# The opening of a decoder trunk in halves: the first conditioning group holds shift and scale of tiles 0 to 3, two weight units do half their products on it, and x is requested ahead of the conditioning weights

## What is computed

```python
def adaln(c, w, b):
    m = jax.nn.silu(c) @ w + b
    return m.reshape(c.shape[0], N_SUB, 3, c.shape[-1])     # shift, scale, gate of each sub-layer
def modulated(x, g, mod, s):
    h = rmsnorm(x, g)
    return h * (1 + mod[:, s, 1][:, None]) + mod[:, s, 0][:, None]
def half_ffn(x, g, mod, s, w_gu, w_down):
    return x + 0.5 * mod[:, s, 2][:, None] * swiglu(modulated(x, g, mod, s), w_gu, w_down)
```

## Time and profile before

| | |
|---|---|
| median of 3 runs | 1281.07 us (1280.49 to 1281.17) |
| profiled execution | 1282.18 us, of which the span from first to last instruction 1280.4 us |
| PE busy | 1231.6 us, 96% of the span |
| DVE, ACT, GpSimd busy | 667.7, 526.6, 131.3 us |
| mean granted TensorE clock | 0.992 |
| read from HBM | 266.55 MB |

### The profile page before, as it was taken

How to read it: one execution, slowest core, us unless ns; L and a number is a source line. 1 busy time by engine, 2 the same in 40 slices (tenths; PEclk the granted TensorE clock), 3 DMA queues, 4 the chain that set the end, 5 groups by cost and what they waited for, 6 DMA issues and landing times.

```text
span 1280.4 us, 23693 instructions
## 1 busy us (share of the span) xinstructions
PE 1231.6 (96%) x9979; PEld 1145.8 (89%) x9979; DVE 667.7 (52%) x986; ACT 526.6 (41%) x722; POOL 131.3 (10%) x124
## 2 busy tenths in 40 slices
PE   5899999999999999999999999999899899999997
PEld 2799999989998999999899999987677499999997
DVE  1644454566675445445545545558645356555553
ACT  1533333343444534333544433355534235554332
POOL 3000001210040000023000001310111040000031
PEclk9999999999999999999999999999999999999998
DMA  9777554568675774355677544584377372544442
GB/s 363 284 292 273 200 218 161 181 203 293 228 281 202 295 288 173 124 171 174 256 263 290 189 139 160 178 310 147 133 284 276 132 263 102 187 163 163 137 158 82
DMA packets 68711, 269.45 MB, mean 210 GB/s; under 512 B 4704, under 2 KB 5152, under 8 KB 54416
## 3 DMA queue, kind: packets, MB, share of 16 engines
q1 hardware_dynamic: 35664, 184.57, 40.0%
q10 hardware_dynamic: 29792, 59.09, 12.6%
q0 software_dynamic: 3168, 24.52, 5.2%
HBM read 266.55 MB, written 1.62 MB: 209 GB/s over the span
## 4 chain that ended last, share of the span: by engine, by line
PE 89%; DVE 4%; DMA 2%; ACT 2%; SPq 1%; issue 0%; ACTq 0%; POOL 0%; DVEq 0%; POOLq 0%
PE bank L1274 25%; PE bank L1275 24%; PE bank L1276 24%; PE bank L1320 3%; PE bank L1560 3%; DMA ada_early<-in_w_ada 1%; PE bank L1573 1%; PE bank L1612 1%; PE bank L1341 1%; ACT w_hi L604 1%; DVE w_lo L825 1%; DMA stage<-in_w_ci 1%; PE bank L1485 1%; DMA stage<-in_w_uq 1%; PE bank L1576 1%; PE bank L1481 1%
## 5 line engine op out<-in xcount | busy, mean ns | idle before, releaser
L825 DVE TENSOR_TENSOR w_lo<-stage,w_hi 128x2048 fp32r<-128x2048 f32 (+2 forms) x182 | 375.0, 2062 | 296.4 <-ACT w_hi L604 295.9
L1274 PE MATMUL bank<-h_hi,w_hi 128*128 128x288 f32 x1608 | 477.5, 297 | 2.8 <-DVE w_lo L825 1.9
L1276 PE MATMUL bank<-h_hi,w_lo 128*128 128x288 f32 x1608 | 475.1, 295 | 0.0
L1275 PE MATMUL bank<-h_lo,w_hi 128*128 128x288 f32 x1608 | 474.5, 295 | 0.0
L604 ACT CAST w_hi<-stage 128x2048 fp32r<-128x2048 f32 (+2 forms) x182 | 304.1, 1674 | 247.8 <-PE bank L1276 171.6
L1274 PEld LDWEIGHTS bank<-h_hi,w_hi 128*128 128x128 f32 x1608 | 302.1, 188 | 7.4 <-issue 3.7
L1275 PEld LDWEIGHTS bank<-h_lo,w_hi 128*128 128x128 f32 x1608 | 302.1, 188 | 0.0
L1276 PEld LDWEIGHTS bank<-h_hi,w_lo 128*128 128x128 f32 x1608 | 302.0, 188 | 0.0
L1275 PE MATMUL bank<-gu_lo,w_hi 128*128 128x288 f32 x768 | 226.6, 295 | 0.0
L1276 PE MATMUL bank<-gu_hi,w_lo 128*128 128x288 f32 x768 | 226.4, 295 | 0.0
L1274 PE MATMUL bank<-gu_hi,w_hi 128*128 128x288 f32 x768 | 225.3, 293 | 0.0
(11 more groups left out here) (233 smaller groups left out, 972.8 us busy)
## 6 DMA issues: line engine op xcount, KB each, us to landing
stage<-in_w_gu SPq DMA_DIRECT2D x88, 1024.0 KB, 4.9
stage_ada<-in_w_ada ACTq DMA_DIRECT2D x53, 1024.0 KB, 9.4
stage<-in_w_down SPq DMA_DIRECT2D x64, 704.0 KB, 4.0
stage<-in_w_ci SPq DMA_DIRECT2D x16, 768.0 KB, 4.5
stage_ada<-in_w_ada SPq DMA_DIRECT2D x9, 1024.0 KB, 10.3
ada_early<-in_w_ada SPq DMA_DIRECT2D x4, 1024.0 KB, 15.0
stage<-in_w_co SPq DMA_DIRECT2D x4, 1024.0 KB, 6.4
stage<-in_w_wo SPq DMA_DIRECT2D x4, 1024.0 KB, 4.9
```

The lines of the kernel that those rows point to most:

```text
L825: nc.vector.tensor_tensor(w_lo[part][:, 0:cols], stage[st_][:, 0:cols], w_hi[part][:, 0:cols], ALU.subtract).then_inc(lo_ready, 1)
L1274: nc.tensor.matmul(out, hi, x_hi, start=start, stop=False)
L1275: nc.tensor.matmul(out, hi, x_lo, start=False, stop=False)
L1276: return nc.tensor.matmul(out, lo, x_hi, start=False, stop=stop)
```

## The change

Group 0 now holds shift and scale of tiles 0 to 3, and group 1 those of tiles 4 to 7. Each quarter comes as two transfers of 512 KB (`half_quarter`), and DVE adds the bias in two instructions a group. x is requested ahead of all conditioning weights, both first weight units ahead of group 1's quarters 0 and 1. The sums of squares and the spread stand between the quarters of group 0 on PE, and the table of the root is loaded early on ACT (`any_root`). `first_norm`, the splits of units 0 and 1, and their products are done in two halves of 4 tiles: the first between group 0 and group 1, the second behind group 1.

```diff
+        def half_quarter(half, q):
+            units = a["w_ada"][0:2 * C_TILES].rearrange("(s u) p (q n) -> p s u q n", s=2, q=RING)
+            return [units[:, s, half * C_TILES // 2:(half + 1) * C_TILES // 2, q, :] for s in range(2)]
...
             sp.dma_start(consts[:], a["consts"]).then_inc(consts_in, 16)
+            sp.dma_start(x[:], a["x"]).then_inc(x_in, 16)
+            def load_half(half, q, into):
+                for s_, src in enumerate(half_quarter(half, q)):
+                    sp.dma_start(by_run(into[q])[:, 2 * s_:2 * s_ + 2], src).then_inc(half_loaded[half][q], 16)
             for q in range(RING):
-                sp.dma_start(by_run(ring[q]), quarter(0, q)).then_inc(ada_loaded[q], 16)
-                if q == 0:
-                    sp.dma_start(x[:], a["x"]).then_inc(x_in, 16)
+                load_half(0, q, ring)
             for q in range(RING):
-                sp.dma_start(by_run(ada_early[q]), quarter(1, q)).then_inc(early_loaded[q], 16)
-                if q == 1:
-                    sp.dma_start(stage[0][:, 0:FLAT[0]], a["w_gu"][0]).then_inc(loaded[0], 16)
+                if q < 2:
+                    sp.dma_start(stage[q][:, 0:FLAT[q]], a["w_gu"][q]).then_inc(loaded[q], 16)
+                load_half(1, q, ada_early)
...
@@ ScalarE @@
-            run("ada_first")
             act.wait_ge(setup_done, 2)
+            nc.scalar.activation(any_root[:], eps[:], ACT.Sqrt)
             root(0)
-            split_hi(0, FLAT[0], 0, 0, 16, False)
-            run("ada_second")
+            after(alone_steps(act, "ada_first")[0])
+            split_half(0, 0)
+            first_norm(0)
+            split_half(0, 1)
+            split_half(1, 0)
+            split_half(1, 1)
+            after(alone_steps(act, "ada_second")[0])
+            first_norm(1)
...
@@ VectorE @@
-            run("ada_first")
             square_last(0)
             inverse_root(0)
-            nc.vector.tensor_tensor(h_fp[:], x[:], rstd.unsqueeze(1).broadcast_to([P, KT, T]), ALU.mult)\
-                .then_inc(hs_step, 1)
-            split_lo(0, FLAT[0], 0, 0)
-            run("ada_second")
+            for half, done in enumerate((half_step, hs_step)):
+                tiles = slice(KT // 2 * half, KT // 2 * (half + 1))
+                nc.vector.tensor_tensor(h_fp[:, tiles], x[:, tiles], rstd.unsqueeze(1)
+                                        .broadcast_to([P, KT // 2, T]), ALU.mult).then_inc(done, 1)
+            after(alone_steps(dve, "ada_first")[1])
+            first_norm(0)
+            split_half(0, 1)
+            split_half(1, 0)
+            split_half(1, 1)
+            after(alone_steps(dve, "ada_second")[1])
+            first_norm(1)
...
@@ TensorE @@
+            def first_units(half):
+                tiles = range(KT // 2 * half, KT // 2 * (half + 1))
+                pe.wait_ge(hs_hi_ready if half else half_hi, 1)
+                for k, st in enumerate(list(steps(pe, SEG["ffn0_gu"], peel_first=True))[0:2]):
+                    pe.wait_ge(lo_ready if half else w_half_lo, k + 1)
...
+                    if k == 0:
+                        pe.wait_ge(hs_ready if half else half_lo, 1)
+                        mm = lagged(outs, parts, tiles, 0)
+                    else:
+                        for kt in tiles:
+                            for g in range(2):
+                                mm = three(outs[g], *parts(kt, g), h_hi[:, kt, :], h_lo[:, kt, :], kt == 0, kt == KT - 1)
+                    if half:
+                        mm.then_inc(unit_used, 1)
...
-            run("ada_first")
-            stats(0)
-            run("ada_second")
+            one_, two_ = alone_steps(pe, "ada_first"), alone_steps(pe, "ada_second")
+            ada_products(one_[0], range(0, 2))
+            stats_sums(0)
+            ada_products(one_[0], range(2, 3))
+            spread(0)
+            ada_products(one_[0], range(3, RING))
+            products(one_[1])
+            first_units(0)
+            products(two_[0])
+            products(two_[1])
+            first_units(1)
```

More of the change, by code:

```diff
@@ L399, in build @@
         loaded = [sem(f"loaded{s}") for s in range(STAGES)]
-        early_loaded = [sem(f"early_loaded{q}") for q in range(RING)]
+        half_loaded = [[sem(f"half_loaded{half}_{q}") for q in range(RING)] for half in range(2)]
         ada_loaded = [sem(f"ada_loaded{q}") for q in range(RING)]
@@ L625, in by_coef, with split_half, first_norm @@
                 nc.scalar.mul(h_fp[:, kt, 0:TP], x[:, kt, 0:TP], coef[:, kt, 0:1]).then_inc(scaled, 1)
+            def split_half(k, half):
+                cols = slice(UNIT // 2 * half, UNIT // 2 * (half + 1))
+                act.wait_ge(loaded[k], 16)
+                nc.scalar.copy(w_hi[k][:, cols], stage[k][:, cols]).then_inc(hi_ready if half else w_half_hi, 1)
+            def first_norm(half):
+                for kt in range(KT // 2 * half, KT // 2 * (half + 1)):
+                    if kt % (KT // 2) == 1:
+                        act.wait_ge(hs_step if half else half_step, 3)
+                        tiles = slice(KT // 2 * half, KT // 2 * (half + 1))
+                        nc.scalar.copy(h_hi[:, tiles, TP:T], h_fp[:, tiles, TP:T])\
+                            .then_inc(hs_hi_ready if half else half_hi, 1)
+                    act.wait_ge(normed, kt + 1)
+                    nc.scalar.activation(h_hi[:, kt, 0:TP], h_fp[:, kt, 0:TP], ACT.Identity,
+                                         bias=mods[:, kt, 0:1]).then_inc(h_hi_ready, 1)
             def norm(n):
@@ L887, in prompt_lo @@
                                                    op0=ALU.add, op1=ALU.subtract).then_inc(h_ready, 1)
[L889 to L893, removed]
-                    .then_inc(hs_step, 1)
[L895 to L900, removed]
+                first = tiles.start
+                dve.wait_ge(step, 1)
+                prompt(first)
+                nc.vector.tensor_tensor(hs4, hs4, by_seq(coef[:, tiles, 1:1 + NSEQ]), ALU.mult).then_inc(step, 1)
+                dve.wait_ge(step, 2)
+                nc.vector.tensor_tensor(hs4, hs4, by_seq(scale_shift(0)[:, tiles, 0, 1:1 + NSEQ]), ALU.add)\
+                    .then_inc(step, 1)
+                if half == 0:
+                    split_half(0, 0)
+                prompt_lo(first)
+                dve.wait_ge(hs_hi_ready if half else half_hi, 1)
+                nc.vector.tensor_tensor(h_lo[:, tiles, TP:T], h_fp[:, tiles, TP:T], h_hi[:, tiles, TP:T], ALU.subtract)\
+                    .then_inc(hs_ready if half else half_lo, 1)
+                for kt in range(first + 1, tiles.stop + 1):
+                    if kt < tiles.stop:
                         prompt(kt)
-                    if kt > 1:
+                    if kt > first + 1:
                         prompt_lo(kt - 1)
@@ L1053, in _ @@
                     norm(n)
-                else:
-                    first_norm()
                 if n == 0:
-                    split_lo(1, FLAT[1], 1, 1)
                     dve.wait_ge(tables_in, 16 * N_TABLES)
```

78 lines of the change are left out of this document (56 added, 22 removed).

## The result

The changed kernel takes **1288.46 us** (median of 5 runs, 1286.9 to 1289.18) where the kernel before takes 1281.17 (5 runs, 1280.49 to 1281.76). The ratio is 1.0058 with a 95% interval from 1.0047 to 1.0068: 7.3 us lost. The forecast was 1285.4, with a range up to 1287.3. Direction and mechanism came as forecast, the size did not.

What follows compares the result with a forecast made beforehand. PE, busy 96% of the span, was taken to bound the kernel. Unit 3 late by 2.7 us plus 1.6 for the clock's fall made 4.3, giving 1285.4 us from the median of 1281.07, range 1280.7 to 1287.3.

Steps and rivals of the forecast that it cites:

- x first, the sums, quarter 3: Opening: GpSimd runs from 7.9 to 18.1, group 0's quarter 3 ends at 25.0, unit 0's first product at 29.7.
- The first halves: Units 0 and 1, first four tiles: unit 0's 24 products take 4.9 us; after group 1, `ada_used` = 2 at 42.0.
- The wait of 0.6 us for unit 1's half: After unit 0's first half, PE waits 0.6 us until DVE has unit 1's first half at 35.2.
- The second halves: Behind group 1: 3.1 us of chain to 45.1, then 48 products in 6.5 to 8.1 us; unit 2 starts between 51.6 and 53.3.
- The queue: SP requests group 2 at 42.0 with unit 3 behind it; unit 3 lands at 58.1 and starts 2.7 us late, at 62.4.
- The clock: Behind PE's wait for unit 3 the clock falls to half rate, costing 0 to 1.7 us, taken as 1.6.
- The sum: Late unit 3 plus clock fall, 2.7 + 1.6 = 4.3 us, applied to the median of 1281.07: 1285.4 us.
- The clock stays: Rival at unit 3: the same 2.7 us stall without the clock's 1.6, time 1283.8; chance 0.24.
- Not slower: Rival: first halves come early enough (`ada_used` = 2 by 39.3) that the stall vanishes, about 1280.2; chance 0.18.
- Later still: Rival: group 1's last quarter lands late or splits queue up, unit 2 waits too, 1 to 2 us more, about 1287; chance 0.14.

Runs made afterwards that it cites:

- the one before with the same delay: Kernel before, nothing in halves, with one SyncE wait added so group 2 is requested only when h's last low part is ready: 1288.67 us, ratio 1.0064.
- the queue mended: Changed kernel with unit 3 requested ahead of the wait for two used groups and of group 2: 1282.68 us, ratio 1.0015.
- the filled halved kernels: Changed kernel, unit 3 requested ahead of group 2, products of ones in PE's gaps before both halves: 1286.02 us; with unit 1's first-half splits earlier, 1283.09 us.
- the best version: Kernel before with unit 1's splits in two halves and nine products of ones in the idle gap ahead of unit 0: 1279.82 us, ratio 0.9988.

## Why the forecast was right in kind and wrong in size

- **x first, the sums, quarter 3.** GpSimd started at 8.19 (7.9 forecast) and ended at 18.64 (18.1); quarter 3 ended at 25.60 (25.0), the first product of unit 0 stood at 29.86 (29.7). These terms were good to 0.6 us, and x first alone changes nothing.
- **The first halves.** 24 products of unit 0 took 5.78 us (29.86 to 35.64), not 4.9: the lower clock held for all of them and not for 16, and the clock lacked 3.4 us there, not the 1.7 of the earlier trace rows. The wait of 0.6 us for unit 1's half that I had added was not needed, so unit 1's half started only 0.4 late. `ada_used` = 2 came at 42.56 instead of 42.0. The second halves began at 46.14 (45.1 forecast) and unit 2 ended at 60.47 (58.1 to 59.8); that cost nothing, because unit 3's `w_lo` was not ready before 63.41.
- **The queue.** Five transfers took 16.5 us from the first request to unit 3's landing (42.63 to 59.15), forecast 16.1. The Trainium skill, page "DMA: Bandwidth & Descriptors", section "Queues, rings and completion order", states that on each DMA engine the descriptors of a ring are consumed in ring order; this case's traces agree, since with unit 3 ahead of the 4 MB the wait of 3.00 us is gone. PE started unit 3 at 63.47 against a forecast of 62.4: a lag of 3.80 instead of **2.7**. Of these 1.1 us half is the later `ada_used`, most of the rest the transfers. The mechanism of this term was right and its size too small.
- **The clock: the step that failed.** I took **1.6** us for it, between 0 and 1.7, from the one stretch in the trace of before, and treated 1.7 as its upper end. It was 2.85 (9.31 less 6.46): the stretch at 0.50 was twice as long as the one in the trace of before. (The recorded "3.4 us of work" at half rate are 3.4 us of time with 1.7 us of work in them; the cost of 1.7 follows from that.) In the opening the clock lacks 1.7 or 3.4 us, and which of the two changes from trace to trace at the same place: in the second halves 1.7 in two traces and 3.4 in three, of programs that are the same or nearly so up to there.
- **The sum.** 3.80 + 2.85 = 6.65, measured at group 2, against 2.7 + 1.6 = 4.3. Of the 3.1 us between forecast and median, 2.35 are these two terms. About 0.3 lies outside the span, which the forecast carried over unchanged: the time is 2.0 to 2.2 us longer than the span in all five runs of the changed kernel, and 1.7 to 1.9 in all runs of the kernel before. The other 0.4 I can't place: the spans of the two traces differ by 5.9 us only, and the profiled execution of before was itself 1.0 us over its median.
- **The rivals.** "The clock stays" is refuted by the traces of the changed kernel and of the one before with the same delay. "Not slower" needed the first halves at the full clock; even with that forced and the queue mended, no halved version beat the kernel before. "Later still" gave the nearest number (1287), but for another reason: no quarter landed late, and unit 2 waited for nothing.

What the halves themselves bring: by the first product of unit 0 they win 7.6 us, by group 2's products nothing is left (66.15 against 66.13 with the queue mended). They don't remove the serial chain from the conditioning sums over ACT, PE, DVE and ACT to the first product, they run it twice: PE stands 4.3 us nearly idle from 25.60 to 29.86 and 3.6 from 42.56 to 46.14, where it stood 3.1 before, and each gap is followed by a stretch at the lower clock. The kernel with the queue mended is still 2.0 us over before by the medians, though its trace is level at 66 us and 0.4 late from 301 us on. Part of it, some 0.2 us, lies outside the span as above, and 1.5 is that the profiled execution of before (1282.18) lay above the median beside it (1280.68); where a typical run of before gains these 1.5 us no trace shows, so it stays open.

## What to carry to other kernels

When a request waits for a semaphore, the requests behind it on that queue wait too, and then stand behind its bytes: before delaying what raises the semaphore, look at the most urgent transfer behind it. PE's stalls of 3.0 and 4.9 us for unit 3 cost their length and then a stretch at half rate, and the size of such a stretch varied from trace to trace, so don't take the one size that a single trace shows as the upper end of a range. And a lead at one place is worth only what the next chain (here the splits on ACT and DVE, later a landing) lets through: idle time ahead of such a place is free, so mend the chain first, and then the idle time; only both together gained here, and narrowly.

## What the runs showed that I had not expected

- In the opening the clock lacks 1.7 or 3.4 us in a stretch and nothing between, and the same place has the one or the other from trace to trace (second halves: 1.7 with unit 3 first, 3.4 with PE kept busy at unit 3). Later in the program there is one of 5.2 (near 1024 us, PE kept busy at unit 3). What PE loses of it depends on what follows: 2.85 of 3.4 at unit 3, next to nothing of 3.4 in unit 0 with x first.
- Filling PE's idle time with useless products keeps the granted clock at 1.00 behind it in every case tried (61, 26, 42 and 35 us), but by itself it bought no time that the medians show, and at 61 and 26 us the products ran 0.6 to 1.0 us past the moment at which PE could have gone on.
- Delays made in the opening were still there at the end by the medians (7.3 and 8.0 us; 5.9 and 3.9 by the spans of the traces), leads of 2.0 and 0.8 us of the filled halved kernels were not: ACT took 1.4 us longer to ask for its own transfers, then a pair of 768 KB transfers landed in 8.6 us instead of 7.3, and the lead became a lag. The lead of 1.3 us of the best version was kept (its span is 1.9 shorter than before's).
